# A hybrid encoder kernel: another order of the dilated heads, early queries and keys, one list of steps at the end

## What is computed

```python
for i in range(2):
    h = rms_norm(x, norm_g[i])
    y = dilated_mixer(h, ...) if i == 0 else mla_mixer(h, ...)
    x = x + y
return rms_norm(x, final_norm_g)
```

## Time and profile before

| | us |
| --- | --- |
| median of 3 runs (lowest, highest) | 1799.57 (1798.11, 1801.09) |
| the profiled execution | 1798.98 |
| its span, first to last instruction | 1797.2 |

### The profile page before, as it was taken

The page is one execution under the profiler, slowest core; times in us unless marked ns, Lnnn a source line. Parts: engine busy times, 40 slices in busy tenths (PEclk is TensorE's granted clock), DMA queues, the critical chain, the costliest instruction groups (busy, mean ns, idle before and its releaser), DMA issues. The chain is left out here.

```text
span 1797.2 us, 24653 instructions
## 1 busy us (share of the span) xinstructions
PE 1722.1 (96%) x8720; PEld 1456.8 (81%) x8720; DVE 1104.8 (61%) x1966; ACT 724.7 (40%) x1465; POOL 409.2 (23%) x328
## 2 busy tenths in 40 slices
PE   6999999999999999999999999689997999999995
PEld 5888888888888888888888888579786888888883
DVE  5354355355456455455545546553887889898996
ACT  5323323323322322322222231342216877877774
POOL 1001001001001000100100100221005777777764
PEclk9999999999999999999999999899998999999998
DMA  4112111111112011112111110021100000000002
GB/s 164 48 35 71 36 36 67 35 41 59 35 35 70 23 47 58 35 35 70 34 36 47 47 50 10 0 90 35 49 0 27 27 27 26 26 26 26 6 7 111
DMA packets 23241, 76.75 MB, mean 43 GB/s; under 512 B 3088, under 2 KB 3216, under 8 KB 22928
## 3 DMA queue, kind: packets, MB, share of 16 engines
q1 hardware_dynamic: 23184, 75.98, 12.4%
HBM read 71.77 MB, written 4.19 MB: 42 GB/s over the span
## 5 line engine op out<-in xcount | busy, mean ns | idle before, releaser
L754 PE MATMUL bankA<-hTh,wh 128*128 128x512 f32 x1280 | 504.5, 394 | 0.4 <-DVE hTl L504 0.4
L754 PE MATMUL bankA<-hTl,wh 128*128 128x512 f32 x1280 | 498.6, 390 | 0.0
L754 PE MATMUL bankA<-hTh,wl 128*128 128x512 f32 x1280 | 498.6, 389 | 0.0
L754 PEld LDWEIGHTS bankA<-hTh,wl 128*128 128x128 f32 x1280 | 240.3, 188 | 50.8
L754 PEld LDWEIGHTS bankA<-hTh,wh 128*128 128x128 f32 x1280 | 240.4, 188 | 48.3 <-issue 1.1
L754 PEld LDWEIGHTS bankA<-hTl,wh 128*128 128x128 f32 x1280 | 240.6, 188 | 47.0
L304 POOL TENSOR_TENSOR prob<-prob,wt_blk 128x1024 f32<-128x1024 f32 x16 | 32.3, 2021 | 1053.6 <-DVE wt_blk L643 1053.6
L554 DVE TENSOR_TENSOR qk<-bankA,qk 128x512 fp32r<-128x512 f32 x96 | 66.4, 692 | 287.1 <-ACT qk L370 286.8
L370 ACT ACTIVATE qk<-bankA 128x512 fp32r<-128x512 f32 x96 | 57.2, 596 | 366.8 <-PE bankA L754 366.8
L530 DVE TENSOR_TENSOR wl<-raw,wh 128x1024 fp32r<-128x1024 f32 x78 | 103.1, 1322 | 14.5 <-ACT wh L340 12.9
L1542 POOL TENSOR_TENSOR probb<-probb,inv 128x512 f32<-128x512 f32 x96 | 100.0, 1042 | 43.5 <-DVE inv L1733 37.6
(11 more groups left out here) (212 smaller groups left out, 3461.7 us busy)
## 6 DMA issues: line engine op xcount, KB each, us to landing
raw<-a_w_in SPq DMA_DIRECT2D x80, 512.0 KB, 3.3
bias<-alibi SPq DMA_DIRECT2D x8, 512.0 KB, 3.3
raw_out<-a_w_out SPq DMA_DIRECT2D x8, 512.0 KB, 4.1
gateT<-b_w_gate SPq DMA_DIRECT2D x8, 512.0 KB, 4.0
raw_o<-b_w_out SPq DMA_DIRECT2D x16, 256.0 KB, 2.6
raw_q<-b_w_q SPq DMA_DIRECT2D x8, 384.0 KB, 3.9
X<-x_prompt SPq DMA_DIRECT2D x4, 512.0 KB, 5.4
X<-x_sample SPq DMA_DIRECT2D x4, 512.0 KB, 8.7
```

What stands on the lines that cost most here:

```text
L754: ins = pe.matmul(proj_ps[b][:, :], w[a][:, slot, k * P:(k + 1) * P], hT[c][:, k, b * S:(b + 1) * S], start=(i == 0), stop=(i == last))
```

## The change

- **Dilated heads.** `PROJ` becomes q0, k0, v0, q1, k1, q2, k2, v1, gate, v2. `ROW_SLOTS` are now k1, q2, k2, v1, so the output rows begin beside (k1,0); `split_out` follows q1. The scores of s1 go beside (k1,1) and (q2,0), those of s2 beside (k2,1) and (v1,0). DVE's `joint_softmax` is cut in three: `gather_sums` (the 16 copies of L629) after q1, ahead of that name's `next_split` and `split_out`; the rest after v1, with ACT's `factors`; `scatter_weights` (the 16 copies of L643) after the gate, ahead of its `next_split`. SP loads the output weights with k0.
- **First pair.** The banks and `ring_done` are shared by both parts of stage B. Behind gate step 2 ACT and POOL split the first pair's query and key/value weights into a free part of `w`; behind the last gate PE computes the four products of `EARLY`. In the heads PE skips them; ACT splits `wkv` ahead of `wq`, and DVE splits `wq` after the takes of `EARLY`.
- **Last pair and end.** `FINAL` replaces pair 7's `ORDER` and `LAST_STEPS`: pair 7's own output rows are "own" steps, three rates ("rate", 0, 4), (4, 6), (6, 8), all eight last scalings on DVE. For units 2 and 3 of pair 7 (`by_vector`) the gate product of "fold" and the low part of "y" move from POOL to DVE.

```diff
-PROJ = ["q0", "k0", "v0", "q1", "k1", "v1", "gate", "q2", "k2", "v2"]
+PROJ = ["q0", "k0", "v0", "q1", "k1", "q2", "k2", "v1", "gate", "v2"]
-ROW_SLOTS = [("gate", 0), ("gate", 1), ("q2", 0), ("q2", 1), ("k2", 0), ("k2", 1), ("v2", 0), ("v2", 1)]
+ROW_SLOTS = [("k1", 0), ("k1", 1), ("q2", 0), ("q2", 1), ("k2", 0), ("k2", 1), ("v1", 0), ("v1", 1)]
...
+            def gather_sums(h):
+
+                dve.wait_ge(exp_done, h * 3 + 1)
+                for s in range(4):
+                    for d in range(4):
+                        ins = dve.tensor_copy(st_tile[32 * d:32 * d + 32, :, s, :], st_blk[32 * s:32 * s + 32, :, d, :])
+                chain(ins, h, 1)
...
+                    if name == "q1":
+                        gather_sums(h)
+                    if name == "gate":
+                        scatter_weights()
                     next_split(h, name)
-                    if name == "v1" and not is_first(h):
+                    if name == "q1" and not is_first(h):
                         split_out(h)
                     if name == "v0":
                         maxima(h, 0, slice(0, NB), at, 0)
-                joint_softmax(h)
+                    if name == "v1":
+                        joint_softmax(h)
...
+                if n == 2:
+                    act.wait_ge(next_loaded, 32)
+                    act.activation(w[HI][:, first_q], keep["raw_q"][:, :], ACT.Copy).then_inc(first_hi, 1)
+                    act.activation(w[HI][:, first_kv], keep["raw_kv"][:, :], ACT.Copy).then_inc(first_hi, 1)
...
+            pe.wait_ge(turn_taken, TR + NB)
+            pe.wait_ge(first_split, 2)
+            for b in range(NB):
+                first_up(2 * b, KQ, first_q.start, cT[0], b)
+                first_up(2 * b + 1, KKV, first_kv.start, cT[1], b)
...
+FINAL = [
...
+    ("score", 3, 2), ("turn", 2, 1), ("score", 3, 3), ("exp", 3, 1), ("exp", 3, 2), ("out", 10), ("weigh", 2, 0),
+    ("norm", 3, 1), ("turn", 2, 2), ("out", 11), ("exp", 3, 3), ("weigh", 2, 1), ("turn", 2, 3), ("norm", 3, 2),
+    ("y", 0), ("norm", 3, 3), ("out", 12), ("out", 13), ("out", 14), ("weigh", 2, 2), ("weigh", 2, 3), ("fold", 2),
+    ("turn", 3, 0), ("turn", 3, 1), ("out", 15), ("y", 1), ("split_out", 1), ("weigh", 3, 0), ("y", 2),
+    ("turn", 3, 2), ("weigh", 3, 1), ("turn", 3, 3), ("own", 0), ("own", 8), ("weigh", 3, 2), ("weigh", 3, 3),
+    ("own", 1), ("fold", 3), ("own", 9), ("own", 2), ("y", 3), ("square", 0), ("own", 10), ("own", 3), ("square", 1),
+    ("square", 2), ("own", 11), ("square", 3), ("own", 4), ("own", 12), ("square", 4), ("own", 5), ("rate", 0, 4),
+    ("own", 13), ("square", 5), ("own", 6), ("final", 0), ("final", 1), ("own", 14), ("own", 7), ("own", 15),
+    ("final", 2), ("square", 6), ("rate", 4, 6), ("final", 3), ("square", 7), ("rate", 6, 8), ("final", 4),
+    ("final", 5), ("final", 6), ("final", 7),
+]
...
+EARLY = [("q_up", 0, 0), ("k_up", 0), ("q_up", 0, 1), ("k_up", 1)]
...
+                        if by_vector(p, s[1]):
+                            dve.wait_ge(o_taken, N + 1)
+                            if s[1] == 2:
+                                dve.wait_ge(y_ready, N)
+                            dve.tensor_tensor(y[rows, b, :], y[rows, b, :], gateT[rows, p, b * S:(b + 1) * S],
+                                              ALU.mult).then_inc(y_ready, 1)
```

More of the change, by code:

```diff
@@ L270, in head @@
                         load_bias(h)
-                    if name == "q1" and not is_first(h):
+                    if name == "k0" and not is_first(h):
                         load_out(h)
@@ L943, in stage_b_in @@
         stat = sb("stat", [P, 3, 2, NT])
-        bank = [ctx.enter_context(nc.psum_tensor(f"bankB{i}", [P, S], F32)) for i in range(8)]
+        bank, ring_done = keep["bank"], keep["ring_done"]
         proj_ps, turn_ps = bank[0:4], bank[4:8]
@@ L1319, in _, with first_up @@
                 gate_rows(g)
+            def first_up(n, ktiles, at, latent_T, b):
+                i, last = 0, len(SPLIT_PRODUCT) * ktiles - 1
+                for k in range(ktiles):
+                    cols = slice(at + 2 * P * k, at + 2 * P * k + P)
+                    for a, z in SPLIT_PRODUCT:
+                        ins = pe.matmul(turn_ps[n][:, :], w[a][:, cols], latent_T[z][:, k, b * S:(b + 1) * S],
+                                        start=(i == 0), stop=(i == last))
+                        i += 1
+                ins.then_inc(ring_done, 1)
+            pe.wait_ge(turn_taken, TR + NB)
[3 more added lines that the diff above has]
+                first_up(2 * b + 1, KKV, first_kv.start, cT[1], b)
 UNITS = ((0, 0), (0, 1), (1, 0), (1, 1))
@@ L1356, in steps_b @@
     return [s for s in ORDER if (prev or not of_previous(s)) and (nxt or s[0] not in ("split_kv", "split_q"))]
-LAST_STEPS = [("y", -4), ("y", -3), ("fold", -2), ("turn", -1, 0), ("turn", -1, 1), ("y", -2), ("weigh", -1, 0), ("turn", -1, 2),
-              ("weigh", -1, 1), ("turn", -1, 3), ("weigh", -1, 2), ("weigh", -1, 3), ("fold", -1),
-              ("y", -1)]
-BESIDE = {4: [("rate", 0)], 5: [("scale", 2), ("final", 0)], 6: [("scale", 3), ("final", 1)]}
-for i_row in range(NT):
-    LAST_STEPS += [("out", i_row), ("out", NT + i_row), ("square", i_row)] + BESIDE.get(i_row, [])
@@ L1368, with at_end @@
+RATES = [s for s in FINAL if s[0] == "rate"]
 RING = 5
-USERS = ("k_up", "q_up", "v_up", "score", "out")
+EARLY = [("q_up", 0, 0), ("k_up", 0), ("q_up", 0, 1), ("k_up", 1)]
+USERS = ("k_up", "q_up", "v_up", "score", "out", "own")
 TURNERS = ("turn", "v_turn")
+def at_end(p):
+    return isinstance(p, int) and p == B_PAIRS - 1
 def places(banks, kinds):
     first, each, last = ([s for s in steps if s[0] in kinds]
-                         for steps in (steps_b(False, True), steps_b(True, True), LAST_STEPS))
+                         for steps in (steps_b(False, True), steps_b(True, True), FINAL))
@@ L1382, in place @@
             return n, n % banks, n // banks
-        n = (last if isinstance(p, int) and p == B_PAIRS else each).index(step)
+        n = (last if at_end(p) else each).index(step)
         slot = n % banks
@@ L1425, in stage_b_heads @@
         junk = prob[:, 0, 2:4, :].rearrange("p t c -> p (t c)")
-        bank = [ctx.enter_context(nc.psum_tensor(f"bankC{i}", [P, S], F32)) for i in range(8)]
+        bank = keep["bank"][4:8] + keep["bank"][0:4]
         ring_ps, turn_ps, o_ps = bank[0:RING], bank[5:7], bank[7]
@@ L1544, in body @@
                         pool.wait_ge(prob_ready, n + 1)
-                    elif s[0] == "fold":
+                    elif s[0] == "fold" and not by_vector(p, s[1]):
                         n = unit(p, s[1])
@@ L1553, in body @@
                         pool.wait_ge(y_ready, n + 1)
-                    elif s[0] == "y":
+                    elif s[0] == "y" and not by_vector(p, s[1]):
                         n = unit(p, s[1])
@@ L1664, in body @@
                         i = s[1]
-                        _, slot, used = ring(p, ("out", NT + i))
+                        _, slot, used = ring(p, ("own", NT + i))
                         act.wait_ge(ring_taken[slot], used + 1)
                         if i == 0:
-                            act.wait_ge(turned, turning(p, ("turn", -1, 0))[0] + 1)
+                            act.wait_ge(turned, turning(p, ("turn", 2, QT - 1))[0] + 1)
                         else:
@@ L1776, in body @@
                 for s in steps:
+                    if first and s in EARLY:
+                        continue
+                    if first and s == ("v_up", 0):
+                        pe.wait_ge(kv_w_split, 1)
                     if s[0] in USERS:
```

141 lines of the change are left out of this document (83 added, 58 removed).

## The result

| | before, run again beside after | after |
| --- | --- | --- |
| median, us (runs) | 1799.2 (20) | 1795.49 (20) |
| lowest, highest | 1798.11, 1801.09 | 1794.61, 1796.64 |
| span of the profiled execution | 1797.2 | 1793.2 |

The ratio is 0.998, its 95% interval 0.9974 to 0.9986. The kernel became faster by 3.7 us of a forecast 9.45: the sign held and the time lies in the range, but the step was two and a half times too large. The profiled execution took 1794.99, 1.8 us more than its span, as before.

A forecast was written before the change was run, and what follows sets the result against it. PE, busy 96% of the span, was taken as the bound. Heads +9.1, last head with its clock -9.45, first pair -1.9 and end -7.2 us summed to -9.45, giving 1790 us, range 1779 to 1798.

The forecast's parts named there:

- The stop in the heads: Heads 1 to 7: PE waits for DVE's split of the output weights before the first output row, 7 x 1.3 = +9.1 us.
- The other moves inside a head I cost at nothing: Repeated heads: moved scores, gates, scatter and load are covered; v2 late by at most 1.6 us in all, entered as nothing.
- The last head: Last dilated head: the wait between v2's turns and the probabilities' turn falls from 13.0 to 4.75 us, gain 8.25.
- Its clock: Behind the last head's shorter stop PE spends less time at half rate: gain 1.2 us (0 to 2.5).
- The first pair: Start of the latent stage: early queries and keys bring the first score 3.2 us earlier, net gain 1.9 (0 to 3.2).
- The end: Last pair and end in one list: own(4) starts earlier, DVE then sets the pace, -7.2 us (-11.3 to -2.3).
- A: Repeated heads: no new stop, as DVE's gather or splits finish before PE asks; 1781 us, chance 14%.
- B: Last pair and end: the single list stops PE and the 7.2 us are lost; 1797 us, chance 12%.
- C: Repeated heads: each new stop drops PE's clock to half rate, 10 to 24 us over seven; 1800 to 1814, chance 7%.

The follow-up runs named there:

- gate_short: The changed kernel with the addition of 1 behind the gate's exp left out in the dilated heads: 1793.69 us, ratio 0.997.
- rows_moved: The changed kernel with the output rows of a head one product later, beside (k1,1), q2, k2, (v1,1) and the gates: 1782.91 us, ratio 0.991.
- gather_late: The changed kernel with DVE's gather_sums behind the split of the output weights instead of ahead of next_split: 1785.33 us, ratio 0.9923.
- gather_half_more: The changed kernel with 8 more copies of gather_sums in each head, into a tile nobody reads: 1807.96 us, ratio 1.0047.
- gather_twice: The changed kernel with 16 more copies of gather_sums in each head, into a tile nobody reads: 1826.59 us, ratio 1.0152.
- last_split_late: The changed kernel with the last head's split of the output weights moved behind the first weighing of its values: 1791.24 us, ratio 0.9955.
- half_final: The changed kernel with DVE's last scalings done on half of each row's columns, the other half stored unscaled: 1793.82 us, ratio 0.9965.

## Why the prediction was wrong in size, step by step

- **The stop in the heads: right in mechanism, size 1.3 forecast, 1.47 measured.** The stop is 1.30 for 1.2, the restart 0.10 for 0.1, and 0.07 of a pass stay without a place. Seven times, 1.2 us.
- **"The other moves inside a head I cost at nothing": the step that failed first.** The gates' lost cover was seen and bounded (0 to 0.1 a request, 1.6 in all), then entered in the sum as 0. It is 0.22 a pass, 1.5 us in seven, the upper bound, as gate_short and rows_moved show. The DVE chain was computed at 5.5 us against 5.44 of PE: a tie, and here it is a stop. Another 0.7 us stand in the first row of the table and belong to head 0 or to the start; the traces' spread there is larger, so the step that left them out can't be blamed for them.
- **The last head: right** (8.6 for 8.25), in mechanism and size: 4.38 us between the turns for 4.75, as the split took 1.86.
- **Its clock: the second failed step.** 1.2 were booked for a shorter stop; 0.0 came back in after, 0.5 on average of the nine traces with such a stop, and 1.8 behind 0.65 us. The forecast took the half rate behind a 3.4 us stop at 1182.3 (3.1 us of it) as the measure for this one. Behind the same 2.9 us stop it lasted 3.5 us in gather_late and 6.8 in after, where 12.0 us had been followed by 6.8 too, so the length of the stop doesn't give the loss.
- **The first pair: right in the chain (3.25 for 3.2, maximum 2.1 for 1.9); the net size is open.** It is 1.6 for 1.9 in the two traces, 0 alone, and the executions differ by more than that.
- **The end: right**, 6.5 for 7.2, with DVE as the bound of the stretch from own(4) to its last instruction; of the 0.7, 0.5 is DVE's wait for POOL's rates.
- **The rivals.** A (no stop) did not come: the seven waits are there. B (stops in the list) neither: three stops, 3.1 us, for 4.1 in the forecast. C did not come at 1.1 us, and the two kernels with more copies show that it is real: in three heads of seven at 2.5 us, in all at 3.9.

In sum, by the two traces, 3.6 of the 5.45 us missed lie in the heads (2.9 of them shown by the passes), 1.2 in the clock, 0.7 in the end, 0.3 in the first pair, less 0.35 won in the last head. By the medians 5.7 were missed (3.7 of 9.45 came).

## What to carry to other kernels

In a loop, an operation whose cover equals its own length is not free: enter the upper bound times the passes, or move something beside it. Ahead of adding a wait look at the instructions in front of it on that engine, and put first the one whose result is asked for first: here one reordering of two neighbouring steps was worth 10 us. And do not scale the clock's loss with the length of a stop: here a stop cut from 12.0 to 2.9 us gave back little more than its length, and cut to 0.65 us its length and the clock.

## What the runs showed of the hardware

- After a stop of 1.1 us PE kept its full clock in seven heads (after); after 2.5 us it fell in three of seven (gather_half_more) and after 3.9 us in all (gather_twice), for 1.6 us of lost time each. After 2.9 us in the last head it fell, for 0.9 to 2.3 us by nine traces, against last_split_late.
- A wait that the profile shows as 1.14 us in front of a product costs 1.47 us of the pass.
- Of the four weighings of a repeated head on POOL (128x1024 each) the first takes 2.93 us in the new order, beside a DVE split, and 1.90 before; in both orders another takes 2.87 to 2.97, and the heads lose nothing by it (rows_moved, with the same 2.93, has the pass of before). The rule of the Trainium skill (SBUF — State Buffer, "Who interferes with whom") that a DVE instruction with two SBUF inputs contends with a GpSimd instruction that reads SBUF fits; no run here separates the port from other causes.
- Four stores of 512 KB rows, issued close together, ran at 406 to 410 GB/s in all (half_final).
